# A second mixer in another order: up products first, attention heads between channel slots, state-space heads between output halves

## The chip, the core and the metric

The kernel runs on one core of one Trainium2 chip. The metric is the device time of one execution in microseconds (us). PE is the matrix engine (TensorE), DVE the VectorE, ACT the ScalarE, POOL the GpSimd engine, SP the engine that issues the weight loads.

## The reference

Two transformer blocks follow each other on 256 tokens of width 1024, in float32. The second is the one that matters here:

```
u = rmsnorm(x, norm_mix_w) @ w_in            # z 1024 | xbc 2048 | dt 16 | q_lat 384 | kv_lat 256 | k_rope 32
xbc = silu(causal_conv4(xbc) + b)            # xs 1024 | B 4x128 | C 4x128
y = (C B^T * exp(segment sums of dt*a)) @ (xs*dt)   # 16 state-space heads of 64
y = group_rmsnorm((y + xs*d_skip) * silu(z))
q = rmsnorm(q_lat) @ w_q_up ; k,v = rmsnorm(kv_lat) @ w_kv_up ; rope on 32 of 96 columns
o = softmax(q k^T / sqrt(96), masked by chunks of 64) @ v    # 16 attention heads of 64
x = x + concat(y, o) @ w_out
x = x + memory_attention(rmsnorm(x), rmsnorm(mem)) ; x = x + conv_ffn(rmsnorm(x))
return rmsnorm(x, norm_final_w)
```

The first block has a mixer of its own (differential attention and retention) and a layer of selected experts.

## The kernel before

The tokens are two halves of 128 partitions (t = 0, 1). All weights stand in DRAM as 463 slots of 128x1024 float32, in the order in which they are used (`order`, `SOURCE`). SP loads them into a ring of three (`ring`). ACT casts a slot to its high part (`w_hi`, `hi_parts`, L1292), POOL forms the rest as `w_lo` (L426, in one stage DVE does), and PE computes each product as three matmuls, high by high, high by low and low by high (L458 to L460). `split` counts slots whose `w_lo` is there, `wait_slot` waits for it on PE, and `spent` counts the slots that PE has finished; ACT may overwrite the parts of a slot when the one three before it is spent. So ACT's place of `hi_parts(n)` in its own list of instructions decides when slot n can be used. PSUM has eight banks of 128x512. The order on every engine is written out by hand, with semaphores between engines.

The second mixer runs on PE in this order. Four slots of dt and q latents, four of kv latents and the k_rope columns, eight of z (`panel`). A product that turns the tokens' norm factors into a row (`row_of`), the transposes of the latents (`turn("latents")`). Then 16 slots of xbc by channels: the input h is unscaled, so DVE first multiplies each result by the row of norm factors, then does the four taps of the convolution, and ACT does Silu on it. Transposes of xs and the group products C B^T stand between and behind them. Then 16 state-space heads: `seg_sum` on PE, `clip` on DVE, Exp on ACT, `weigh` on DVE (L2504), three matmuls on PE. Between them stand the up products of q and kv (`up`, 17 units of six 512-column matmuls, nine slots, copied out by ACT and DVE in `up_copied`) and the rotation of q (`rope_products`, `rope_sums` on DVE). Then the transposes of q and k (`qk_turn`), 16 attention heads (`mla_scores`, `masked` on DVE, `mla_exp` on ACT, `mla_turn`, copies, `mla_out`, L1063) with 13 halves of the output product between them (`out_half`, 12 matmuls of 512 columns each, state-space part first), the transposes of the attention output (`out_turn`), and the remaining halves. `add_residual` adds four banks to x on DVE (L1957), and transposes for the next norm follow (L497).

In the last lines DVE multiplies the second half of x by factor and gain as one 128x1024 instruction (L2718) and SP stores it as one transfer of 512 KB, while ACT does the same for the first half.

## Time and profile before

| | us |
|---|---|
| three runs | 1583.86 (median), 1579.18, 1587.04 |
| profiled execution | 1582.71 |
| its span | 1580.6 |
| PE busy | 1508.9 (95%) |
| DVE, ACT, POOL busy | 850.8, 752.0, 971.7 |
| mean granted PE clock | 0.987 |

Busy times are of the span. A matmul's shown length is longer than the distance to the next one's start, since matmuls are pipelined, and so a busy PE isn't a PE at its peak. The second mixer is the stretch from 1064.5 to 1309.9.

### The profile page before, as it was taken

To read this page: it belongs to the slowest core of one execution; us is meant where nothing else is said; L and a number is where in the kernel's file an instruction comes from. 1 tells how busy PE (TensorE), PEld (TensorE's weight loads), DVE (VectorE), ACT (ScalarE), POOL (GpSimd) and SP (SyncE) were. 2 spreads that over 40 slices of the span, in tenths; PEclk is the share of its full clock that TensorE was granted. 3 is DMA by queue.
4 is the path that set the end of the run, shared out by engine and by line. 5 is a ranking of instruction groups with operands and counts; after the bars stand their busy time and mean duration, and the time that the engine had idled before them with its cause. 6 is when DMAs were issued, how large, how long until landed. Compare 5 with 4: busy or idle time off the path is not lost.

```text
span 1580.6 us, 26597 instructions
## 1 busy us (share of the span) xinstructions
PE 1508.9 (95%) x9602; PEld 1354.5 (86%) x9602; DVE 850.8 (54%) x2090; ACT 752.0 (48%) x1248; POOL 971.7 (61%) x412
## 2 busy tenths in 40 slices
PE   7998999999999999999999999979997999999997
PEld 6677999989998888899999999968975878899996
DVE  4555289999996655422222222255776523365665
ACT  6465545544444545444444444455435545544443
POOL 7547888855553000288888888877741155588885
PEclk9999999999999999999999999999997999999999
DMA  7334556543335566565555555554521044355553
GB/s 248 122 105 140 180 180 234 187 134 108 121 108 160 187 195 192 181 187 187 187 187 186 186 186 186 186 196 152 185 83 51 28 173 148 120 163 186 185 185 119
DMA packets 69200, 254.15 MB, mean 161 GB/s; under 512 B 7744, under 2 KB 8000, under 8 KB 68480
## 3 DMA queue, kind: packets, MB, share of 16 engines
q1 hardware_dynamic: 67104, 244.35, 48.6%
q10 hardware_dynamic: 1584, 6.68, 1.2%
q0 software_dynamic: 432, 2.07, 0.3%
q8 instruction: 50, 0.82, 0.2%
q14 instruction: 30, 0.25, 0.0%
HBM read 249.91 MB, written 3.15 MB: 160 GB/s over the span
## 4 chain that ended last, share of the span: by engine, by line
PE 31%; issue 31%; POOL 27%; DVE 8%; POOLq 1%; DMA 1%; ACT 0%; DVEq 0%; ACTq 0%
POOL w_lo L426 27%; PE bank L458 9%; PE bank L459 9%; PE bank L460 9%; PE bank L851 4%; DVE arena L2219 1%; DVE arena L2216 1%; DVE arena L2218 1%; DMA ring<-weights_in 1%; DVE arena L2217 1%; DVE arena L2287 1%; DVE arena L2285 1%; DVE arena L2288 1%; DVE arena L2215 1%; POOLq L436 0%
## 5 line engine op out<-in xcount | busy, mean ns | idle before, releaser
L426 POOL TENSOR_TENSOR w_lo<-ring,w_hi 128x1024 fp32r<-128x1024 f32 x403 | 968.4, 2406 | 593.3 <-ACT w_hi L1292 586.2
L1292 ACT CAST w_hi<-ring 128x1024 fp32r<-128x1024 f32 x460 | 482.4, 1050 | 639.3 <-PE bank L460 595.4
L458 PE MATMUL bank<-h_hi,w_hi 128*128 128x256 f32 x1696 | 487.5, 287 | 5.4 <-ACT arena L1780 2.3
L460 PE MATMUL bank<-h_hi,w_lo 128*128 128x256 f32 x1696 | 480.4, 283 | 0.0
L459 PE MATMUL bank<-h_lo,w_hi 128*128 128x256 f32 x1696 | 480.3, 283 | 0.0
L458 PEld LDWEIGHTS bank<-h_hi,w_hi 128*128 128x128 f32 x1696 | 325.4, 192 | 10.3 <-POOL w_lo L426 2.6
L459 PEld LDWEIGHTS bank<-h_lo,w_hi 128*128 128x128 f32 x1696 | 325.5, 192 | 3.6
L460 PEld LDWEIGHTS bank<-h_hi,w_lo 128*128 128x128 f32 x1696 | 325.2, 192 | 0.0
L458 PE MATMUL bank<-w_hi,act_hi 128*128 128x512 f32 x600 | 235.0, 392 | 4.6 <-DVE act_lo L2372 1.7
L459 PE MATMUL bank<-w_lo,act_hi 128*128 128x512 f32 x600 | 234.5, 391 | 0.0
L460 PE MATMUL bank<-w_hi,act_lo 128*128 128x512 f32 x600 | 233.5, 389 | 0.0
L2367 DVE TENSOR_TENSOR bank<-bank,arena 128x256 f32<-128x256 f32 x68 | 29.4, 433 | 278.2 <-ACT bank L1598 278.1
L458 PEld LDWEIGHTS bank<-w_hi,act_hi 128*128 128x128 f32 x600 | 113.0, 188 | 27.0 <-issue 4.0
L460 PEld LDWEIGHTS bank<-w_hi,act_lo 128*128 128x128 f32 x600 | 112.7, 188 | 24.3
L459 PEld LDWEIGHTS bank<-w_lo,act_hi 128*128 128x128 f32 x600 | 113.0, 188 | 20.1
L2341 DVE TENSOR_TENSOR w_lo<-ring,w_hi 128x1024 fp32r<-128x1024 f32 x60 | 73.5, 1225 | 67.4 <-ACT w_hi L1292 67.2
L458 PE MATMUL bank<-w_hi,h_hi 128*128 128x512 f32 (+2 forms) x224 | 92.9, 415 | 16.7 <-POOL w_lo L426 13.5
L460 PE MATMUL bank<-w_hi,h_lo 128*128 128x512 f32 (+2 forms) x224 | 87.5, 390 | 0.0
L459 PE MATMUL bank<-w_lo,h_hi 128*128 128x512 f32 (+2 forms) x224 | 87.4, 390 | 0.0
L2310 DVE TENSOR_SCALAR work<-bank,chosen_t 128x128 f32<-128x128 f32 x256 | 86.9, 401 | 0.0
L458 PEld LDWEIGHTS bank<-w_hi,h_hi 128*128 128x128 f32 x224 | 43.5, 194 | 31.7 <-POOL w_lo L426 19.0
L851 PE MATMUL bank<-work 128*128 128x128 f32 x512 | 67.4, 275 | 0.0
(392 smaller groups left out, 1836.9 us busy)
## 6 DMA issues: line engine op xcount, KB each, us to landing
ring<-weights_in SPq DMA_DIRECT2D x463, 512.0 KB, 3.5
mem_kv<-arena ACTq DMA_DIRECT2D x2, 1024.0 KB, 7.0
arena<-mem_kv ACTq DMA_DIRECT2D x2, 1024.0 KB, 6.2
xres<-x_in SPq DMA_DIRECT2D x2, 512.0 KB, 6.6
arena<-mem_in POOLq DMA_DIRECT2D x1, 1024.0 KB, 7.9
arena<-rows_in ACTq DMA_DIRECT2D x2, 512.0 KB, 5.2
arena<-consts_in POOLq DMA_DIRECT2D x1, 512.0 KB, 8.7
arena<-consts_in ACTq DMA_DIRECT2D x2, 256.0 KB, 6.3
```

The costliest lines, as they stand in the source:

```text
L426: nc.gpsimd.tensor_tensor(w_lo[:, k, :], ring[:, k, :], w_hi[:, k, :].bitcast(F32), ALU.subtract)\
L458: pe.matmul(out_, a[0], b[0], start=start, stop=False, **kw)
L459: pe.matmul(out_, a[0], b[1], start=False, stop=False, **kw)
L460: return pe.matmul(out_, a[1], b[0], start=False, stop=stop, **kw)
L851: mm = pe.matmul(bank[:, g % 3, i * P:(i + 1) * P], one_hots(2 + u)[:, i, :], one_hots(u)[:, i, :], start=True, stop=True)
L1292: nc.scalar.copy(w_hi[:, k, :], ring[:, k, :]).then_inc(s["hi_made"], 1)
L2215: link(v.max(top[:, 0:8], values))
L2216: v.max_index(index[:, 0:8], top[:, 0:8], values)
L2217: link(v.match_replace(rest, top[:, 0:8], values, -3.0e38))
L2310: v.tensor_scalar(one_hots(u)[:, i, :], iota_p, of(0), of(2), ALU.is_equal, ALU.mult)\
L2341: v.tensor_tensor(w_lo[:, k, :], ring[:, k, :], w_hi[:, k, :].bitcast(F32), ALU.subtract)\
L2367: v.tensor_tensor(a, a, g, ALU.mult).then_inc(s["act_product"], 1)
```

## The change

- The order of the second mixer's slots becomes dt and q, kv and k_rope, z, q_up, kv_up, xbc, output. The channels of xbc come in another order (`XBC`: two of the groups' B and C by turns first, then xs), and in the output product the attention half comes first.
- The latents are transposed between the two panels of z. All 17 up units run one after the other, in banks 6, 7 and 4, 5 by turns. Between the nine of q and the eight of kv PE does 16 transposes of x scaled by its norm factor (`x_mix`, one half scaled by ACT, one by DVE), whose high and low parts (`mix_h`) are the input of the xbc slots. The row of factors and DVE's 16 multiplications by it go.
- Each attention head has one xbc slot between `mla_turn` and `mla_out` (heads 0 to 13; two slots stand ahead), with the group products, transposes of xs and of the attention output at fixed heads (`CB_AT`, `XS_AT`, `OUT_AT`). DVE does the convolution of a slot in each head; ACT does Silu in batches of four at every fourth head. Scores are scaled in ACT's copy of q and masked in PSUM, on 256 columns.
- The state-space heads come last, ten of them with half an output slot of the attention half (`HALF_AT`), six halves follow, then the transposes of y and the 16 halves of the state-space part. y is summed and gated in four groups instead of two halves. The loads of the memory keys and values from DRAM (ACT's queue) move to the eighth state-space head.
- Additions by banks: where PE signalled after two banks of a product, it now signals after banks 0, 1 and 2, and DVE's four additions wait one by one (`residual_half`, four uses, and `mixer_half`).
- First mixer: some of ACT's casts (`hi_parts`) take other places in its list. With `hi_parts(m)` ACT casts all slots up to m that it hasn't cast yet.
- End: squares, gain and factor are done in four pieces of 128x512, and the output goes out in four transfers of 256 KB.

```diff
+XBC = [8, 12, 9, 13, 10, 14, 11, 15] + list(range(8))
...
-    order = ["w_in", "w_out", "mem_k", "queries", "mem_v", "experts", "dt_q", "kv_rope", "z", "xbc", "q_up", "kv_up",
+    order = ["w_in", "w_out", "mem_k", "queries", "mem_v", "experts", "dt_q", "kv_rope", "z", "q_up", "kv_up", "xbc",
...
+        elif name == "xbc":
+            stage(name, [SLOT[name] + j for j in XBC])
+        elif name == "w_out_2":
+            stage(name, [SLOT[name] + (k + KD) % (2 * KD) for k in range(2 * KD)])
...
+XS_AT = {12: (0, 0, 7), 13: (1, 0, 3)}
+OUT_AT = {6: 0, 10: 1, 14: 2}
+HALF_AT = (0, 2, 3, 4, 6, 7, 8, 10, 11, 12)
...
             low("norm_mix", 7)
             panel("z", 0, 512, 0)
-            panel("z", 1, 512, 2)
-            pe.wait_ge(s["mix_scale"], 1)
-            row_of((bank[:, 7, :], 0))
+            pe.wait_ge(s["copied_act"], c0 + 1)
+            pe.wait_ge(s["copied_dve"], d0 + 1)
             pe.wait_ge(s["latents_scaled"], 1)
             turn("latents", lambda b, t: lat[:, t, 16 + b * P:16 + (b + 1) * P] if b < 3 else
                  lat[:, t, 512 + (b - 3) * P:512 + (b - 2) * P], 5, bank0=4)
...
                 name, c, depth, k = UP[i]
-                if k == 0 and i:
-                    before = 3 * (name == "kv_up") + c
-                    pe.wait_ge(s["copied_act"], COPY["q_up"][0] + before)
-                    pe.wait_ge(s["copied_dve"], COPY["q_up"][1] + before)
-                n, half, mm = up_unit(name, c, depth, k, lat_t, 3 * (name == "kv_up"), 512, 6)
...
                 elif i == 2:
                     mm.then_inc(s["up_first"], 1)
-            pe.wait_ge(s["cum_copied"], 1)
-            for i in range(3):
+            for i in range(9):
                 up(i)
-            for g in range(SG):
-                pe.wait_ge(s["xbc_silu"], 13 + g)
-                pe.wait_ge(s["conv_done"], 4 * (13 + g))
+            pe.wait_ge(s["copied_act"], z0 + 4)
+            pe.wait_ge(s["norm_scaled"], SCALED["mix"])
+            turn("mix_h", lambda b, t: x_mix[:, t, b * P:(b + 1) * P], KD)
+            for i in range(9, len(UP)):
+                up(i)
+            adt = area("dts")[:, 0:32].rearrange("p (t h) -> p t h", t=TT)
...
-                if h:
-                    pe.wait_ge(s["mla_masked"], h)
+                if h >= 2:
+                    pe.wait_ge(s["mla_exp"], h - 1)
+                to = 4 - 2 * (h % 2)
...
+            low("mix_h", KD - 1)
+            xbc(0)
+            pe.wait_ge(s["rotated"], TT)
+            pe.wait_ge(s["copied_act"], COPY["kv_up"][0] + 4)
+            pe.wait_ge(s["copied_dve"], COPY["kv_up"][1] + 4)
+            for i in range(4):
+                qk_turn(i, 4 + i)
+            xbc(1)
+            mla_scores(0)
+            mla_scores(1)
+            pe.wait_ge(s["qk_out_act"], 4)
+            for h in range(MH):
+                if h + 2 < MH:
+                    mla_scores(h + 2)
+                mla_turn(h)
+                if 4 + h < MH:
+                    pe.wait_ge(s["qk_out_act"], 4 + h)
+                    qk_turn(4 + h, 7)
+                if 2 + h < 16:
+                    xbc(2 + h)
+                if h == 0:
+                    cum()
+                if h in CB_AT:
+                    cb_product(CB_AT[h])
+                if h in OUT_AT:
+                    pe.wait_ge(s["cb_masked"], (2, 4, 4)[OUT_AT[h]])
+                    if h == 14:
+                        pe.wait_ge(s["xdt_made"], 2)
+                    out_turn(OUT_AT[h], 3)
+                if h in XS_AT:
+                    if h == 12:
+                        pe.wait_ge(s["qk_out_act"], MH)
+                    else:
+                        low("mla_out", 3)
+                    xs_turn(*XS_AT[h])
+                mla_out(h)
...
-                if i == 4 * KD - 2:
-                    mm.then_inc(s["residual_half"], 1)
+                    if k == 2 * KD - 1 and 2 * t + h < 3:
+                        mm.then_inc(s["residual_half"], 1)
...
+            seg_sum(0)
+            seg_sum(1)
+            xs_turn(0, 1, 7)
+            low("mla_out", 5)
+            xs_turn(1, 1, 3)
+            out_turn(3, 2)
...
+            for h in range(SH):
+                if h in HALF_AT:
+                    if done == 1:
+                        low("mla_out", 7)
+                        pe.wait_ge(s["xdt_made"], 4)
+                    out_half(done, m_t)
...
+                if h == 0:
+                    pe.wait_ge(s["xdt_made"], 2)
+                    pe.wait_ge(s["mla_out_copied"], 4)
+                if h == 4:
+                    pe.wait_ge(s["xdt_made"], 4)
+                if h in (8, 12):
+                    pe.wait_ge(s["y_ready"], h // 4 - 1)
...
+                    seg_sum(h + 2)
             while done < 2 * KD:
-                out_half(done, h_t)
+                out_half(done, m_t)
                 done += 1
-            pe.wait_ge(s["mla_out_copied"], 4)
-            out_turn(3, 6)
+            pe.wait_ge(s["y_ready"], SG)
+            pe.wait_ge(s["y_scaled"], 2 * TT)
+            turn("ssd", lambda b, t: xs[:, t, b * P:(b + 1) * P], KD, bank0=4)
             for i in range(2 * KD, 4 * KD):
-                out_half(i, m_t, lambda k: low("mla_out", k))
+                out_half(i, h_t, lambda k: low("ssd", k))
...
-            hi_parts(24 + NS)
+            hi_parts(25 + NS)
...
-            hi_parts(25 + NS)
             mem_k_copied(0)
+            hi_parts(26 + NS)
             act.wait_ge(s["head_mean"], 2)
...
-            hi_parts(26 + NS)
+            hi_parts(27 + NS)
...
-            hi_parts(29 + NS)
+            hi_parts(28 + NS)
...
+            hi_parts(STEP["z"] + 1 + NS)
...
+            act.wait_ge(s["norm_factor"], NORMS["mix"] + 1)
+            nc.scalar.mul(x_mix[:, 0, :], xres[:, 0, :], rstd[:, 6:7]).then_inc(s["norm_scaled"], 1)
...
-            turned_hi("latents", lat_t, 5, lambda b: col("q_g", b) if b < 3 else col("kv_g", b - 3), bank0=4)
-            for j in range(16):
-                hi_parts(STEP["xbc"] + j + 1 + NS)
-                act.wait_ge(s["conv_done"], 4 * (j + 1))
-                nc.scalar.activation(xc[:, j, :], xc[:, j, :], ACT.Silu).then_inc(s["xbc_silu"], 1)
-                if j in (10, 14):
-                    b = j // 14
-                    act.wait_ge(s["turned"], TURN["xs"][0] + 2 * b + 1)
-                    nc.scalar.copy(xs[:, 0, b * 512:(b + 1) * 512], bank[:, 7 - 2 * b, :]).then_inc(s["turned_out_act"], 1)
+                if c == 0:
+                    turned_hi("latents", lat_t, 5, lambda b: col("q_g", b) if b < 3 else col("kv_g", b - 3), bank0=4)
...
+            for p in range(3):
+                up_copied(p)
+            turned_hi("mix_h", h_t, 4, lambda b: col("mix_g", b))
+            up_copied(3)
+            turned_hi("mix_h", h_t, 4, lambda b: col("mix_g", 4 + b), first=4, skip=4)
+            for p in range(4, 7):
+                up_copied(p)
...
+            M = STEP["xbc"] + NS
+            hi_parts(M + 1)
+            for i in range(4):
+                qk_out(i, 4 + i)
+            nc.scalar.activation(warm[:, 6:7], ident[:, 0:1], ACT.Exp)
+            hi_parts(M + 2)
             mla_exp(0)
             mla_exp(1)
             for h in range(MH):
+                if 4 + h < MH:
+                    qk_out(4 + h, 7)
                 if h + 2 < MH:
                     mla_exp(h + 2)
-                if 4 + h < MH:
-                    qk_out(4 + h, 7)
-                if h == 1:
-                    turned_hi("ssd", h_t, KD, lambda b: col("ssd_g", b))
-                if h >= 3:
-                    hi_parts(STEP["w_out_2"] + (h - 3) // 2 + NS)
...
+                if h % 4 == 3:
+                    for pos in range(h - 3, h + 1):
+                        act.wait_ge(s["conv_done"], 4 * (pos + 1))
+                        x = xc[:, XBC[pos], :]
+                        nc.scalar.activation(x, x, ACT.Silu).then_inc(s["xbc_silu"], 1)
+                if 2 + h < 16:
+                    hi_parts(M + 3 + h)
+                if h in OUT_AT:
+                    out_hi(OUT_AT[h], 3)
...
+            O = STEP["w_out_2"] + NS
+            done = 0
+            for h in range(SH):
+                act.wait_ge(s["seg_clipped"], 2 * (h + 1))
+                b = bank[:, 4 + h % 2, 0:3 * P]
+                nc.scalar.activation(b, b, ACT.Exp).then_inc(s["seg_exp"], 1)
+                if h == 0:
+                    out_hi(3, 2)
+                if h in HALF_AT:
+                    hi_parts(O + done // 2)
+                    done += 1
+                if h in (6, 10, 14):
+                    y_squares((h - 6) // 4)
+                if h == 7:
+                    act.wait_ge(s["xdt_made"], 4)
+                    act.dma_start(area("mk_t"), mem_kv[:, 0, :]).then_inc(s["mem_kv_loaded"], 16)
+                    act.dma_start(area("mv"), mem_kv[:, 1, :]).then_inc(s["mem_kv_loaded"], 16)
...
+            hi_parts(O + 8)
+            turned_hi("ssd", h_t, KD, lambda b: col("ssd_g", b), bank0=4)
...
+            piece = lambda a, i: a[:, i // 2, i % 2 * 512:i % 2 * 512 + 512]
+            for i in range(4):
+                act.wait_ge(s["residual_added"], 4 * USE["ffn"] + i + 1)
+                nc.scalar.activation(squares[:, i % 2 * 512:i % 2 * 512 + 512], piece(xres, i), ACT.Square, scale=0.03125,
+                                     accum_out=ssq[:, i:i + 1]).then_inc(s["norm_summed"], 1)
+                act.wait_ge(s["norm_summed"], 2 * NORMS["final2"] + i + 1)
+            act.wait_ge(s["norm_mean"], NORMS["final2"] + 1)
+            nc.scalar.activation(rstd[:, 4:6], ssq[:, 4:6], ACT.Sqrt).then_inc(s["norm_rooted"], 1)
...
-            act.wait_ge(s["gained"], 1)
-            nc.scalar.mul(out_sb[:, 0, :], out_sb[:, 0, :], rstd[:, 2:3]).then_inc(s["out_ready"], 1)
-            act.wait_ge(s["out_ready"], 1)
-            act.dma_start(out[:, 0, :], out_sb[:, 0, :]).then_inc(s["out_stored"], 16)
-            act.wait_ge(s["out_stored"], 32)
+            for n, i in enumerate((2, 0)):
+                nc.scalar.mul(piece(out_sb, i), piece(out_sb, i), rstd[:, 6 + i // 2:7 + i // 2]).then_inc(s["out_ready"], 1)
+                act.wait_ge(s["out_ready"], n + 1)
+                act.dma_start(piece(out, i), piece(out_sb, i)).then_inc(s["out_stored"], 16)
+            act.wait_ge(s["out_stored"], 64)
...
                     for h in range(2):
+                        if 2 * t + h < 3:
+                            dve.wait_ge(s["residual_half"], 3 * use + 2 * t + h + 1)
+                        else:
+                            dve.wait_ge(s["spent"], spent)
                         v.tensor_tensor(xres[:, t, h * 512:(h + 1) * 512], xres[:, t, h * 512:(h + 1) * 512],
                                         bank[:, 2 * t + h, :], ALU.add).then_inc(s["residual_added"], 1)
...
+            v.tensor_scalar(x_mix[:, 1, :], xres[:, 1, :], rstd[:, 7:8], None, ALU.mult).then_inc(s["norm_scaled"], 1)
...
+            for p in range(3):
+                up_copied(p)
+            mix_lo(0)
+            mix_lo(1)
+            rope_products(0)
+            up_copied(3)
+            rope_sums(0)
+            mix_lo(2)
+            mix_lo(3)
+            up_copied(4)
+            rope_products(1)
+            rope_sums(1)
+            up_copied(5)
+            up_copied(6)
...
+                b = bank[:, 4 - 2 * (h % 2), :]
+                causal = b.rearrange("p (t c) -> p t c", t=TT)[:, :, 0:P]
+                v.tensor_tensor(causal, causal, mask.unsqueeze(1).broadcast_to([P, TT, P]), ALU.add).then_inc(s["mla_masked"], 1)
                 dve.wait_ge(s["mla_masked"], h + 1)
...
+            def conv(pos):
+                j = XBC[pos]
+                dve.wait_ge(s["spent"], STEP["xbc"] + pos + 1)
+                b = bank[:, pos % 2, :]
+                v.tensor_scalar(xc[:, j, :], b[:, 0:T], col("xw", 4 * j + 3), col("xb", j), ALU.mult, ALU.add)\
+                    .then_inc(s["conv_done"], 1)
+                for d in range(1, 4):
+                    dve.wait_ge(s["conv_done"], 4 * pos + d)
+                    v.scalar_tensor_tensor(out=xc[:, j, d:T], in0=b[:, 0:T - d], scalar=col("xw", 4 * j + 3 - d),
+                                           in1=xc[:, j, d:T], op0=ALU.mult, op1=ALU.add).then_inc(s["conv_done"], 1)
...
+                if h - 1 in OUT_AT:
+                    out_lo(OUT_AT[h - 1], 3)
+                if 1 + h < 16:
+                    conv(1 + h)
+                if h == 0:
+                    dve.wait_ge(s["cum_done"], 1)
+                    v.tensor_copy(dts[:, 64:96], bank[:, 3, 0:32])
+                    v.tensor_copy(area("cum_t")[0:SH, :], bank[0:SH, 3, T:2 * T]).then_inc(s["cum_copied"], 1)
+                if h in CB_AT:
+                    cb_mask(CB_AT[h])
+                if h in XS_AT:
+                    xs_out(h - 12, *XS_AT[h])
...
+                dve.wait_ge(s["ssd_out"], 4 * g + 4)
+                b = bank[:, 6 + g % 2, :].rearrange("p (t c) -> p t c", t=TT)
+                a = xs[:, :, g * 256:(g + 1) * 256]
+                link(v.tensor_tensor(b, b, a, ALU.add))
+                v.tensor_tensor(a, b, z[:, :, g * 256:(g + 1) * 256], ALU.mult).then_inc(s["y_ready"], 1)
...
+                if h == 0:
+                    xs_out(3, 1, 1, 3)
+                    out_lo(3, 2)
+                    dve.wait_ge(s["xdt_made"], 4)
+                if h in (5, 9, 13):
+                    y_group((h - 5) // 4)
...
+            piece = lambda a, i: a[:, i // 2, i % 2 * 512:i % 2 * 512 + 512]
+            gain = lambda i: area("final_g")[:, i % 2 * 512:i % 2 * 512 + 512]
+            for i in (2, 0):
+                v.tensor_tensor(piece(out_sb, i), piece(xres, i), gain(i), ALU.mult).then_inc(s["gained"], 1)
+            dve.wait_ge(s["norm_summed"], 2 * NORMS["final2"] + 4)
...
+            for i in (3, 1):
+                v.scalar_tensor_tensor(out=piece(out_sb, i), in0=piece(xres, i), scalar=rstd[:, 6 + i // 2:7 + i // 2], in1=gain(i),
+                                       op0=ALU.mult, op1=ALU.mult).then_inc(s["half_ready"], 1)
```

## Rows read from the trace of the kernel before

**Rows 1.** The page, first line.

```profile
span 1580.6 us, 26597 instructions
```

**Rows 2.** Windows by stage: length, busy time (instructions) by engine, granted clock, DMA share, GB/s.

```profile
1064.50:1094.00 29.50, 26.34 (x111) 21.43 (x111) 10.71 (x24) 17.39 (x28) 21.47 (x10) 0.88 0.51 166
1094.00:1146.90 52.90, 49.78 (x414) 48.92 (x411) 42.58 (x91) 26.23 (x41) 40.37 (x17) 1.00 0.55 170
1146.90:1207.50 60.60, 53.18 (x246) 40.36 (x247) 43.15 (x99) 24.38 (x47) 22.19 (x10) 0.95 0.27 85
1207.50:1235.20 27.70, 20.99 (x103) 17.72 (x104) 15.18 (x35) 15.86 (x49) 0.00 (x0) 0.68 0.01 5
1235.20:1285.70 50.50, 48.62 (x301) 41.37 (x300) 24.01 (x60) 22.61 (x65) 14.32 (x6) 1.00 0.20 63
1285.70:1309.90 24.20, 22.62 (x100) 17.92 (x98) 1.96 (x4) 11.32 (x13) 20.36 (x9) 1.00 0.69 243
```

**Rows 3.** Timeline of PE in an attention head: start, duration, instructions.

```profile
1241.00 0.88 PE L1063 MATMUL bank<-arena,work 128*128 128x64 f32 x6 [0.44 <-DVE work L2605]
...
1243.11 0.48 PE L458 MATMUL bank<-w_hi,h_hi 128*128 128x512 f32 x1
1243.43 0.40 PE L459 MATMUL bank<-w_lo,h_hi 128*128 128x512 f32 x1
1243.66 0.40 PE L460 MATMUL bank<-w_hi,h_lo 128*128 128x512 f32 x1
```

**Rows 4.** Waits, 1020 to 1300: total us, times, longest.

```profile
PE bank L458 <- POOL w_lo L426: 11.7, 10, 3.2
```

**Rows 5.** Windows of the lower clock, columns as in rows 2.

```profile
1214.80:1228.70 13.90, 12.15 (x48) 9.91 (x47) 6.06 (x16) 8.46 (x26) 0.00 (x0) 0.51 0.00 0
```

**Rows 6.** Timeline of PE behind the output product.

```profile
1311.40 1.20 PE L497 MATMUL bank<-cst,xres 128*128 128x128 f32 x9 [0.27 <-DVE xres L1957]
```

**Rows 7.** Timeline of PE among z's first slots.

```profile
1076.06 0.79 PE L458 MATMUL bank<-w_hi,h_hi 128*128 128x512 f32 x1 [3.16 <-POOL w_lo L426]
```

**Rows 8.** Timeline of ACT ahead of it.

```profile
1069.48 1.28 ACT L1659 ACT_TABLE_LOAD   x1
1070.77 0.23 ACT L1659 ACTIVATE arena<-arena 128x32 f32<-128x32 f32 x1
...
1072.56 2.92 ACT L1292 CAST w_hi<-ring 128x1024 fp32r<-128x1024 f32 x3
```

**Rows 9.** Timeline of DVE, the rotation of k.

```profile
1073.49 0.17 DVE L1982 TENSOR_TENSOR arena<-arena,rope 128x16 f32<-128x16 f32 x1
1073.69 2.35 DVE L1983 TENSOR_TENSOR arena<-arena 128x16 f32<-128x16 f32 x1
```

**Rows 10.** Timeline of POOL at that time.

```profile
1073.66 7.20 POOL L426 TENSOR_TENSOR w_lo<-ring,w_hi 128x1024 fp32r<-128x1024 f32 x3 [4.58 <-ACT w_hi L1292]
```

**Rows 11.** Timeline of DVE in the state-space heads.

```profile
1203.51 0.62 DVE L2504 TENSOR_TENSOR arena<-bank,arena 128x256 f32<-128x256 f32 x2 [1.30 <-ACT bank L1709]
1204.04 0.88 DVE L2494 TENSOR_SCALAR bank<-bank,arena 128x128 f32<-128x128 f32 x2
1205.49 0.62 DVE L2504 TENSOR_TENSOR arena<-bank,arena 128x256 f32<-128x256 f32 x2 [0.57 <-ACT bank L1709]
```

**Rows 12.** Timeline of PE, a state-space head until the next unit.

```profile
1198.31 0.43 PE L1022 MATMUL bank<-arena 128*128 128x64 f32 x2 [2.22 <-DVE arena L2504]
...
1199.75 0.50 PE L458 MATMUL bank<-w_hi,lat_hi 128*128 128x512 f32 x1
```

**Rows 13.** Waits in the first mixer, 110 to 150.

```profile
PE bank L458 <- POOL w_lo L426: 2.5, 1, 2.5
...
PE bank L458 <- DVE h_lo L1914: 2.0, 1, 2.0
```

**Rows 14.** Timeline of DVE: the additions, and the last instruction.

```profile
1308.70 2.65 DVE L1957 TENSOR_TENSOR xres<-xres,bank 128x512 f32<-128x512 f32 x4 [19.37 <-PE bank L460]
...
1574.98 1.28 DVE L2718 SCALAR_TENSOR_TENSOR arena<-xres,rstd,arena 128x1024 f32<-128x1024 f32 x1
```

521 lines of the change are left out of this document (219 added, 302 removed).

## The prediction

> **How the profile was read, and what bounds the kernel.** First the page: the span of the profiled execution is 1580.6 us [rows 1], and that execution took 1582.71 us, so 2.1 us lie outside the span. It is 1.15 us under the median of the three runs, 1583.86. I work against its time, and the prediction needs no correction beyond that. 0.5% is 7.9 us: a median under 1576.0 counts as faster, one over 1591.8 as slower.
>
> Then the table by stages of the second mixer, which the change rewrites [rows 2]: dt, kv, rope and z until 1094.0, the 16 channel (xbc) slots until 1146.9, the state-space heads with the up products until 1207.5, the passage to attention until 1235.2, the attention heads with output halves until 1285.7, the rest of the output product until 1309.9. In each, PE is the busiest engine, yet it is busy for 221.5 of 245.4 us. What is to be had is what PE loses, and it loses in three ways:
> - Idle: 3.2, 3.1, 7.4, 6.7, 1.9 and 1.6 us by stage, 23.9 in all [rows 2].
> - Restarts. Running 512-column matmuls start 0.23 apart though each is shown for 0.40, so each stop costs about 0.16 more [rows 3]. PE stops some 25 times, for POOL, DVE or ACT (ten times for POOL in the stretch of [rows 4]): 4.0.
> - Half clock. The stretch at 1214.8 was granted 0.51, the lower level, 1.2 GHz [rows 5]. From the mean grants 0.88, 0.95 and 0.68 [rows 2], the time at that level is 2 x 0.12 x 29.5 + 2 x 0.05 x 60.6 + 2 x 0.32 x 27.7 = 30.9 us, and with PE busy 0.76 to 0.89 of it, half of that work was lost: 3.2 + 2.7 + 6.7 = 12.6. Ahead of the 1214.8 stretch PE waited for DVE again and again.
>
> Losses before: 40.5. The mixer's work at full speed is then 245.4 - 40.5 = 204.9.
>
> **The change in the second mixer.** Work added on PE: 16 transposes of the scaled x and no row product, 1.8 - 0.6 = +1.2 (nine transposes are shown for 1.20, of which about 0.3 is the last one's own length: 0.11 each [rows 6]; the row product is estimated at five such matmuls). The sum now asks what PE loses in the new order.
>
> *Up to z's fourth slot.* PE waited 3.16 for POOL at 1076.06 [rows 7], because ACT did Exp and Ln with two table loads ahead of three casts [rows 8], and POOL stood without w_hi. The change puts two casts first, so this wait goes. The two loads (1.28 each) and the new scaling of x now delay a later slot; PE, 2.73 a slot (12 x 0.228) against POOL's 2.40, has won 0.3 a slot by then. Left: 1.6 (0 to 3.2).
>
> *Up products alone, 17 units.* A unit is six matmuls, 1.37; with the transposes 25 us for nine slots, and POOL needs 9 x 2.40 = 21.6, so it keeps up, barely. Formerly the same units filled the waits of the state-space heads. What is late next is DVE: copies, mix_lo and both rope halves stand in one queue, and PE needs its copies for the bank of two units on. 1.3 for that. The rope sums and products read two SBUF tiles; one such small op takes 0.17, and 2.35 when it met POOL's w_lo [rows 9, 10]. Of twelve I let two meet it where PE waits, 1.5 each. Left: 4.3 (0 to the rival below).
>
> The Trainium skill, page "SBUF — State Buffer", section "Who interferes with whom", says that a VectorE instruction with two SBUF inputs and a GpSimd instruction reading SBUF hold each other off for a whole instruction. The 2.35 beside 0.17 agrees. It speaks against putting rope beside nine w_lo in a row, and is what rival B stands on.
>
> *Attention heads with an xbc slot each.* PE: a head is 2.11 (1241.00 to 1243.11), a slot is 24 matmuls of 256 columns, half of 0.23 each and rounded up to 0.12, 2.88 [rows 3]: 4.99. DVE: the heads with halves took 24.01/16 = 1.50, the slots 42.58/16 = 2.66 [rows 2], 4.2 together, and 3.7 without the row scaling, one of a slot's five operations (0.5 at most). ACT: 22.61/16 + 26.23/16 = 3.05, and with eight more table loads (two for each batch of four Silus) 8 x 1.28/16 = 0.64: 3.7. POOL 2.4. So PE sets the pace, and the 3.1 idle of the slots and the 1.9 of the heads go. At the first head the chain scores, mask, maxima, exp has little cover: 2.0 (0 to 4).
>
> The Trainium skill, page "ScalarE: Activation LUTs", section "What ACT_TABLE_LOAD costs", adds to each load a drain of about its own length. In this trace the next activation comes right behind the load and nothing stands before it, 1069.48 to 1070.77 [rows 8]. By the page ACT would be at 4.4 a head instead of 3.7, and the sum stays what it is.
>
> *From the last head to state space.* Heads 14 and 15 have no slot: 2.11 on PE against about 3.7 on DVE and ACT, twice 1.6: 3.2. Then DVE has a queue: two clips (0.88 each), the division and two products for xs (0.66 each, as the bank-wide additions of [rows 14]) and the first weigh (0.62), 4.4, and ACT's hand-over, 1.30 [rows 11]. Against these 5.7 PE has twelve transposes (1.3) and one half (2.7): 1.7 is open, and about 1.1 for the transposes that wait for the division. Left 6.0 (2 to 9).
>
> *State-space heads with halves.* PE alone takes 1.44 a head (1198.31 to 1199.75) [rows 12], DVE 1.98 (1203.51 to 1205.49) [rows 11]. Ten heads have a half, 2.73 more on PE, and are PE's. The other six are DVE's: 6 x 0.54 = 3.2. The group sums (two operations, 1.3) stand in front of the next weigh three times: 3.9. Head 0's extra DVE work past its half: 0.7. Left 7.8 (3 to 12).
>
> *The state-space half of the product last.* Six halves (16.4) now lie between the last head and the turn, and hide the norm (squares, root, factor, scaling) whose place was in the 6.7 idle of 1207.5 to 1235.2. If that cover were gone, some 5 would come back. Left 0.7.
>
> *Clock.* The long stretches at the lower level stood where PE waited in short steps, in the two passages. One such, 7 us long at busy 0.85, is put in for the passage to state space: 3.0 (0 to 7).
>
> Losses after, restarts in them: 1.6 + 4.3 + 2.0 + 6.0 + 7.8 + 0.7 + 3.0 = 25.4. Change in the mixer: 25.4 + 1.2 - 40.5 = -13.9.
>
> *Costed at nothing:* the order of the slots in DRAM and the ring (the same loads in another order); the loads of memory keys and values moved to the eighth state-space head, which compete with at most five weight loads while the DMA engines were busy 0.20 and 0.69 of the last two stages [rows 2]; q scaled in ACT's copy (same instruction); the mask on 256 columns instead of 384 (off PE's path, in DVE's 3.7).
>
> **The other parts.** *First mixer:* casts for the slots ahead are moved in front of ACT's waits. PE waits there 2.5 for POOL once and 2.0 for DVE's h_lo once [rows 13]. If both went 4.5 would come, but h_lo waits on the same ACT, one cast later: -3.0 (-4.5 to +1, a cast of 1.05 in front of what PE waits for). *Additions by bank, five places:* DVE adds 4 x 0.66 (2.65 from 1308.70), PE waits 0.27 behind it [rows 6, 14]. Now bank 1's add needn't wait for bank 0's pair and bank 2's starts a quarter earlier; at three boundaries a turn follows at once: -0.8 (0 to -1.5). *Tail:* the last product by DVE is 1.28 at 1024 wide, and the DMA waits for all of it [rows 14]; by halves 0.64 of it is hidden behind the first transfer, and squares by pieces save some more, while four signals cost some: -0.9 (0 to -1.5).
>
> **Sum.** -13.9 - 3.0 - 0.8 - 0.9 = -18.6: span 1562.0, time 1564.1.
>
> **Rivals.**
> A, the new stalls are mostly absent (chance 0.18). For it: PE's six stages of before had only 1.6 to 7.4 idle each. Passage 2 and not 6, state-space heads 4 and not 7.8, first head 1, up products 1: 12.1 less, and about 2 from the clock: 1550.
> D, DVE or ACT paces the attention heads (0.08). Each head has four hand-overs PE, DVE, ACT, PE, and two batches of Silu stand in ACT's queue before a cast that POOL and so the slot wait for. At 5.9 a head instead of 4.99, 14 heads: +12.6, 1577. Against it: the sums 3.7 and 3.7.
> B, the port (0.04): all twelve rope operations meet a w_lo and PE waits for all: 12 x 2.2 - 3.0 = +23.4, 1587.5. Against it: with POOL idle they run at full speed, and before, one or two in a row met it, not all. It would take ten waits more than the two counted to undo the gain.
> C, the clock, on the slower side (0.05): PE falls to the lower level in the passage to state space, and waits for DVE in six of 16 heads keep it there to the end of the six further halves. 16 x 1.44 + 10 x 2.73 + 6 x 2.73 = 66.7 of work; at half clock it takes as much again, less the stalls (7.8) and clock loss (3.0) already counted, and less about a fifth as ten heads have long busy runs: +40, 1604. It decides from 20 us of full-speed work done at half clock beyond what is counted. For it: 1214.8 to 1228.7 was such a passage [rows 5]; against: there PE had no product, and with halves (1235.2 on) the grant was 1.00 [rows 2].
> That the change does nothing: not possible for 40 us of reordered losses, but gain and loss may cancel; it lies in D and B.
>
> **Chances and range.** Forecast 0.65, A 0.18, D 0.08, C 0.05, B 0.04. The forecast's own range follows from its bounds taken together in part: 1556 to 1573. Over all, 1546 to 1580 leaves out C, B, the lower third of A and the far ends of the rest, under 2 in 10. Faster: forecast and A, 0.83. Within: D and B, and some of what reaches past the forecast's end, 0.10. Slower: C and the end of B, 0.07.
>
> **What would show it.** Right: no 3 us wait for POOL at z's first slots, a shorter one near its fifth; attention heads with a slot 5.0 apart and PE over 0.95 busy; a gap of 4 to 8 us and a drop of the grant before the first state-space head; heads without a half 2 apart, later after a group sum; the mixer from the dt slots to the last half about 231.5 long. Wrong: heads 5.5 or more apart with PE waiting for DVE or ACT (D); rope operations of 2.4 with PE behind them (B); a grant near 0.5 over the state-space heads (C); an up-product stage with POOL as PE's releaser.

## The result: 1559.86 us, 1.6% faster

| | before | changed |
|---|---|---|
| median (lowest to highest) | 1583.04 (1579.18 to 1587.04), 4 runs | 1559.86 (1555.44 to 1560.11), 4 runs |
| profiled execution, its span | 1582.71, 1580.6 | 1555.44, 1553.6 |

The ratio is 0.9844, with a 95% interval of 0.9826 to 0.9862. That is 22 to 28 us less; 18.6 were forecast. By the rule of 0.5% in the prediction it counts as faster. The profiled execution of the changed kernel was its fastest, so differences between the two traces flatter it by some us, and the experiments below take that apart.

Windows by stage of the changed kernel: until the second panel of z, the up products, the attention heads with xbc slots, the state-space heads with halves, the rest of the output product (columns as in [rows 2]):

```profile
1059.30:1088.90 29.60, 28.60 (x129) 23.26 (x130) 14.11 (x31) 22.84 (x37) 25.27 (x11) 1.00 0.59 185
1088.90:1114.00 25.10, 23.61 (x125) 19.89 (x124) 15.96 (x31) 14.80 (x27) 20.70 (x9) 1.00 0.61 188
1114.00:1205.00 91.00, 87.35 (x684) 82.97 (x683) 65.66 (x154) 57.82 (x129) 38.31 (x17) 0.98 0.32 99
1205.00:1255.00 50.00, 47.53 (x215) 36.71 (x214) 30.97 (x80) 19.03 (x43) 12.51 (x6) 0.86 0.28 95
1255.00:1283.00 28.00, 27.20 (x128) 22.52 (x127) 7.96 (x13) 14.15 (x23) 22.52 (x10) 1.00 0.50 154
```

The five windows are 223.70 long and PE is busy in 214.29 of it. The same stretch took 245.4 [rows 2]. PE's idle time in it is 9.4, where it was 23.9. Its waits from the last up units on, grouped:

```profile
PE bank L1153 <- DVE arena L2660: 2.5, 2, 1.4
PE bank L1036 <- ACT work L1754: 1.6, 1, 1.6
PE bank L1056 <- DVE work L2629: 1.3, 1, 1.3
PE bank L1066 <- issue: 0.8, 1, 0.8
PE bank L470 <- DVE h_lo L1978: 0.8, 1, 0.8
```

And the two of the stages before, among z's slots and at the fifth panel of the up products, in PE's timeline:

```profile
1072.86 0.50 PE L470 MATMUL bank<-w_hi,h_hi 128*128 128x512 f32 x1 [0.88 <-POOL w_lo L438]
...
1107.63 0.47 PE L470 MATMUL bank<-w_hi,lat_hi 128*128 128x512 f32 x1 [1.42 <-issue]
```

An attention head with its slot is 4.96 long, from one `mla_out` to the next (4.99 forecast), and there is no gap between. The heads that also have a group product or transposes of the attention output are 5.40 to 5.84 long:

```profile
1137.29 0.78 PE L1056 MATMUL bank<-arena,work 128*128 128x64 f32 x6
1137.90 0.87 PE L1036 MATMUL bank<-arena 96*128 96x128 f32 x4
...
1142.25 0.78 PE L1056 MATMUL bank<-arena,work 128*128 128x64 f32 x6
```

What was not so small is the clock. Windows of the changed kernel: the passage to state space, two heads later, the last heads, and the stretch behind the first memory query product:

```profile
1200.00:1208.00 8.00, 6.91 (x25) 5.44 (x26) 6.08 (x16) 4.73 (x10) 0.00 (x0) 0.60 0.21 66
1220.00:1228.00 8.00, 8.00 (x35) 6.11 (x33) 5.30 (x14) 3.36 (x9) 2.36 (x1) 0.79 0.39 131
1244.00:1252.00 8.00, 6.30 (x22) 5.29 (x23) 3.59 (x10) 4.72 (x12) 2.38 (x1) 0.62 0.03 7
1293.00:1298.00 5.00, 3.95 (x21) 3.95 (x22) 0.00 (x0) 1.95 (x3) 4.19 (x2) 0.66 0.33 94
```

In the mixer 17 us ran at the lower level (31 before). The last row is new: PE waits 2.27 there as before, and here the grant fell for 3.4 us behind it. The stretch from the additions behind the output product to the next ones is 68.52 in this trace. Of the thirteen traces of the changed kernel and its variants, four have this fall and are 68.52 to 68.63 long there. Eight others are 67.13 to 67.17, and the one with the old additions, without the fall, is 67.74, as before. So 1.4 of the gain were given back.

The grant didn't only fall behind stops. In the middle of the state-space heads it fell while PE was busy all the time:

```profile
1222.00:1224.00 2.00, 2.00 (x6) 1.59 (x5) 1.87 (x5) 1.59 (x6) 1.21 (x1) 0.52 0.00 0
```

### The profile page after: what moved, and what is told of

Same layout as the page of the kernel before. It is cut to its first block, busy times and chain, and to the rows that moved or that the text cites. A ratio compares the mean times of both kernels' runs of the same rounds, so it can differ in the third digit from the quotient of the medians.

```text
span 1553.6 us, 26642 instructions
## 1 busy us (share of the span) xinstructions
PE 1500.3 (97%) x9614; PEld 1351.3 (87%) x9614; DVE 848.3 (55%) x2085; ACT 763.1 (49%) x1267; POOL 972.1 (63%) x412
## 4 chain that ended last, share of the span: by engine, by line
PE 31%; issue 30%; POOL 28%; DVE 8%; POOLq 1%; DMA 1%; ACT 1%; DVEq 0%; ACTq 0%
POOL w_lo L438 28%; PE bank L470 9%; PE bank L471 9%; PE bank L472 9%; PE bank L861 4%; DVE arena L2283 1%; DVE arena L2280 1%; DVE arena L2282 1%; DVE arena L2281 1%; DMA ring<-weights_in 1%; DVE arena L2351 1%; DVE arena L2349 1%; DVE arena L2352 1%; DVE arena L2279 1%; POOLq L448 0%
## 5 line engine op out<-in xcount | busy, mean ns | idle before, releaser
L470 PE MATMUL bank<-w_hi,h_hi 128*128 128x512 f32 (+2 forms) x224 | 89.5, 400 | 13.5 <-POOL w_lo L438 11.0
```

Of the source, the lines that this page charges most:

```text
L470: pe.matmul(out_, a[0], b[0], start=start, stop=False, **kw)
```

## The experiments

An execution of one and the same kernel varies by up to 10 us here, more than most edits are worth. So each profiled execution is also cut at marks that all kernels have: the first addition behind the first mixer, those ahead of and behind the second mixer, and so on. "The mixer" below is the stretch from DVE's additions ahead of the second mixer's norm to those behind its output product: 272.85 in the trace of before, 251.19 in that of the changed kernel. The time at the lower clock is twice the missing grant times the length, and the idle time is the sum of PE's gaps. Each ratio is against runs of the kernel before made in the same group, whose medians are 1582.68 to 1584.6; across groups the ratios compare better than the times.

### The changed kernel again, and its three small parts undone

> The changed kernel again, as the base of this group. The theory of the trace: its profiled execution (1555.44) was its fastest, and in the others one stretch more is done at the lower clock, so the median comes out near 1559 and the ratio to the kernel before near 0.984. If the profiled execution was typical and the others disturbed, the median is near 1556.

Measured: 1561.09 (1552.05 to 1562.69), ratio 0.9851 (0.9825 to 0.9878). The first profiled execution was a lucky one, as the first theory said. The profiled execution of this group has a span of 1558.9, and 27.3 us of its mixer at the lower clock where the first had 17.1.

Casts of the first mixer in their old places:

```diff
-            hi_parts(25 + NS)
+            hi_parts(24 + NS)
...
-            mem_k_copied(0)
-            hi_parts(26 + NS)
+            hi_parts(25 + NS)
+            mem_k_copied(0)
...
-            hi_parts(27 + NS)
+            hi_parts(26 + NS)
...
-            hi_parts(28 + NS)
+            hi_parts(29 + NS)
```

> Only the order of ACT's casts in the first mixer is put back. Theory: that order is worth what the two traces differ by at the end of the first mixer, 3.8 us, so this kernel is 3 to 4.5 us slower than the changed one. Rival: of the 3.8 a part is clock (0.95 against 1.00 granted there) that comes and goes by execution, and only the 2.1 of idle time is the order's: 2 us slower.

Measured: 1559.83, ratio 0.9861 (0.9838 to 0.9884), no difference that the times can tell. The traces tell it. The additions behind the first mixer start at 146.39; in the changed kernel's trace at 143.22, and at 142.75 to 145.04 in all twelve with the new order. PE's waits in that mixer with the old places, and then in the changed kernel:

```profile
PE bank L470 <- POOL w_lo L438: 2.5, 1, 2.5
PE bank L470 <- DVE h_lo L1978: 1.7, 1, 1.7
```

```profile
PE bank L697 <- DVE arena L2232: 1.2, 1, 1.2
PE bank L470 <- POOL w_lo L438: 1.1, 1, 1.1
```

4.2 of waits against 2.3. The order is worth 3.2 by these two traces, of which 1.9 is waits and the rest clock and restarts: the old order's trace has 3.4 us at the lower clock there. The trace of before has the old order too. Its additions start at 147.52, of which 0.7 is the wait for a second bank, so 146.8 is the number to compare. Against the mean of the twelve traces with the new order, 143.5, the two old ones are 3.1 later, and single pairs differ by 1.3 to 4.1.

Additions with the old waits:

```diff
-                        if 2 * t + h < 3:
-                            dve.wait_ge(s["residual_half"], 3 * use + 2 * t + h + 1)
+                        if t == 0:
+                            dve.wait_ge(s["residual_half"], 3 * use + 2)
```

> Only the additions wait as before (banks 0 and 1 for bank 1, banks 2 and 3 for the last). Theory: 0.27 of PE's wait at each of three boundaries comes back, 0.8 us slower, at most 1.5. Rival: the wait in front of the second half of the transposes is paid by nobody else, and it is 0 to 0.3.

Measured: 1556.57, ratio 0.9845 (0.9821 to 0.9869). Again only the marks tell: from the additions behind the output product to those behind memory attention 67.74 against 67.15 in the run beside it, from there to the last additions 193.92 against 193.31, and from PE's last matmul to the end 9.53 against 8.97 (8.97 in the first trace too, and 9.26 before; the expectations' 8.94 and 9.31 come from spans rounded to 0.1). So it is 0.6 at each of three places, 1.8 in all. The edit changes two more places, at the end of the first mixer and of the experts. The stretches there differ by 2 us and more from trace to trace, so nothing can be read from them. PE's last product and the transposes behind memory attention, in the changed kernel:

```profile
1351.31 0.39 PE L472 MATMUL bank<-w_hi,m_lo 128*128 128x512 f32 x1
1351.54 2.14 PE L509 MATMUL bank<-cst,xres 128*128 128x128 f32 x16
```

All 16 transposes run through, where nine of them waited 0.27 for DVE [rows 6]. The 0.27 was only part of it: the first seven had also stood apart.

The end as before, in two pieces (SP's part of the edit; ACT's squares and scaling and DVE's gain and factor go back with it):

```diff
-            for n, i in enumerate((3, 1)):
-                sp.wait_ge(s["half_ready"], n + 1)
-                sp.dma_start(out[:, i // 2, i % 2 * 512:i % 2 * 512 + 512], ...
+            sp.wait_ge(s["gained"], 2)
+            sp.dma_start(out[:, 1, :], out_sb[:, 1, :]).then_inc(s["out_stored"], 16)
```

> Only the last part is put back: gain, factor and transfer in two pieces of 512 KB. Theory by the two traces: from the start of PE's last matmul to the end of the span it was 9.31 us before and 8.94 after, so 0.4 slower. The prediction's term was 0.9. Rival: the four smaller transfers cost as much as they gain, 0.

Measured: 1557.59, ratio 0.9833 (0.9808 to 0.9858). From PE's last matmul to the end 8.67, against 8.97 with four pieces: the pieces cost 0.30, and what the end gained it gained from the additions. The last rows of ACT in the changed kernel show where:

```profile
1547.84 0.72 ACT L1933 ACTIVATE arena<-arena,rstd 128x512 f32<-128x512 f32 x1 [0.29 <-DVE rstd L2810]
1548.59 0.36 ACTq L1935 DMA_DIRECT2D out<-arena  x1
1549.00 0.72 ACT L1933 ACTIVATE arena<-arena,rstd 128x512 f32<-128x512 f32 x1 [0.44 <-ACT arena L1933]
1549.75 0.34 ACTq L1935 DMA_DIRECT2D out<-arena  x1
```

ACT scales one piece, issues its transfer, and only then scales the other. The last transfer leaves 5.09 after PE's last matmul began (1544.66); before it was 5.00 (1576.29 and 1571.29). This trace of the two-piece end also had the mixer at 252.67, with a stop of 3.76 among the up products in place of 1.42. That was the lead for the third group.

### Stops and the clock in the state-space heads

Two more halves among the heads, ahead of the matmuls of heads 13 and 14, so that four remain behind them:

```diff
-HALF_AT = (0, 2, 3, 4, 6, 7, 8, 10, 11, 12)
+HALF_AT = (0, 2, 3, 4, 6, 7, 8, 10, 11, 12, 13, 14)
```

> Two of the six halves that stood behind the state-space heads move to heads 13 and 14, where PE stopped for DVE's weigh (1.39 and about 0.9). Theory 1, the lower clock follows such stops: both stops go and with them the stretch of about 7 us at the lower clock that began at the second in all five traces, so the stretch from the additions before the mixer to those behind it shrinks by 2.3 + 3 = 5 us. Theory 2, the clock falls with the thin matmuls of these heads, stops or not: only the 2.3 of the stops, and a stretch at the lower clock stands there as before. Rival to both: with four halves left the norm of the state-space output is late and PE waits up to 2 us at its transposes.

Measured: 1554.56 (1551.41 to 1559.45), ratio 0.9822 (0.9794 to 0.985). PE's timeline of the changed kernel at the last two heads, 14 and 15, and then the windows of this one there:

```profile
1244.62 0.43 PE L1153 MATMUL bank<-arena 128*128 128x64 f32 x2 [1.40 <-DVE arena L2660]
...
1246.58 0.69 PE L1153 MATMUL bank<-arena 128*128 128x64 f32 x2 [1.08 <-DVE arena L2660]
...
1248.89 0.63 PE L472 MATMUL bank<-w_hi,m_lo 128*128 128x512 f32 x1
```

```profile
1240.00:1248.00 8.00, 8.00 (x39) 6.02 (x39) 5.45 (x14) 3.37 (x8) 3.61 (x2) 1.00 0.34 81
1248.00:1256.00 8.00, 7.16 (x37) 5.74 (x35) 5.06 (x8) 6.13 (x15) 2.40 (x1) 1.00 0.12 51
```

A 512-column matmul shown for 0.63 is one at the lower level. Both stops are gone and so is the stretch of 6.8 us at that level, which began at or between the two stops in each of the ten traces that have them. It is absent in all three traces that have the halves there. From the first matmul of head 12 to the additions behind the output product, the same work took 40.24 to 41.05 in the ten (mean 40.53) and 36.56 or 36.57 in the three. That is 4.0 less: more than theory 2's 2.3, and near theory 1's 5 with the rival's wait taken off. That wait came, but small: 1.57 at the transposes, where it was 0.79. Of the 4.0 the stops are 1.2 (2.2 gone in the mean, 1.0 new), and the 2.8 that are left are what 6.8 us of lower clock cost. So the clock came back with the stops. What isn't separated: the edit also puts wide matmuls between the thin ones of these heads, and a run of thin matmuls together with a stop could do the same as the stop alone.

Stops aren't the whole rule either. In six of the thirteen traces the grant fell once more among the first state-space heads, for 3.4 to 13.7 us, with no stop of over 0.15 directly ahead (one is the row at 1222.00 above). What brings that is open.

Three edits ahead of these heads: the convolution of the last slot goes behind DVE's last copy, the second transposes of xs to bank 7 (three waits of PE that go with it are left out here), and an up copy ahead of two low parts.

```diff
-XS_AT = {12: (0, 0, 7), 13: (1, 0, 3)}
+XS_AT = {12: (0, 0, 7), 13: (1, 0, 7)}
...
-                if 1 + h < 16:
-                    conv(1 + h)
+                if h < 14 or h == 15:
+                    conv(min(1 + h, 15))
...
+            up_copied(4)
             mix_lo(2)
             mix_lo(3)
-            up_copied(4)
```

> Three edits that take away stops ahead of the state-space heads: DVE does the last convolution behind the last copy (stop of 1.26), the second xs transposes go to bank 7 and so the transposes of the attention output needn't wait for DVE (stop of 0.83), and DVE copies an up product ahead of two low parts (stop of 1.43, in one trace 3.76). Theory 1 (stops bring the lower clock): 3.5 us by the stops and 3 to 6 by the clock behind the passage. Theory 2: the 3.5 alone, the stretch at the lower clock in the first state-space heads stays.

Measured: 1561.02 (1554.07 to 1569.31), ratio 0.9849 (0.9816 to 0.9882): neither theory. The stops of the passage moved instead of going (0.83 and 1.25 became 0.82, 0.65 and 0.96), so whether the clock there follows them was not tested. The worst stop was 6.00, at the transposes of q and k behind the up products, instead of 1.42 among them.

> Both together, and the end (gain, factor, transfer) as before in two pieces of 512 KB, which by the traces is 0.26 shorter (8.71 against 8.97 from PE's last matmul to the end). Theory 1: -5 -6.5 -0.3, near 1547 and under 0.978 of the kernel before. Theory 2: -2.3 -3.5 -0.3, near 1553.

Measured: 1556.35 (1551.97 to 1561.17), ratio 0.9832 (0.9805 to 0.9858); the grant stayed at 1.00 over the last heads here too, and the passage kept three stops (0.82, 0.65 and 1.27) and 6.8 us at the lower level. A miss as a whole: no better than the two halves alone.

### What paces the attention heads

Silu in each head (`if True: for pos in (h,):` in place of `if h % 4 == 3: for pos in range(h - 3, h + 1):`).

> Silu of a slot in every attention head instead of four in every fourth: the same activations, and ACT changes its function table 32 times for the 8 of the changed kernel. ACT has 3.05 of work a head and now two loads. By the row (1.28 a load, no drain) 3.05 + 2.56 = 5.6 a head, 0.6 over PE's 4.97: 16 x 0.6, about 10 us slower. By the page of the Trainium skill, ScalarE: Activation LUTs, 2.66 a switch, an estimate: 3.05 + 5.32 = 8.4 a head, 54 us slower. If ACT's queue is no chain at all but is hidden by the two heads that it runs ahead: 0.

Measured: 1563.7 (1558.41 to 1566.92), ratio 0.9867 (0.9829 to 0.9905). Windows over the same 77 us of heads, first this kernel and then the changed one:

```profile
1127.70:1204.70 77.00, 76.16 (x612) 73.43 (x613) 57.44 (x133) 72.72 (x129) 31.75 (x14) 1.00 0.29 90
```

```profile
1121.20:1198.20 77.00, 76.14 (x611) 73.43 (x612) 57.20 (x133) 46.76 (x108) 32.69 (x15) 1.00 0.31 97
```

The heads are as long as in the changed kernel (69.01 from the first `mla_out` to the fourteenth in both), and ACT is busy 26.0 more for 21 more loads, 27 instead of 6, 1.24 each. My 3.05 of other ACT work was too much: it is 46.76 in the 77 us, 3.0 a head with the loads. So even the crowded ACT, 4.7 a head, stayed under PE's 4.97. At 2.66 a switch, the figure of the Trainium skill (ScalarE: Activation LUTs, What ACT_TABLE_LOAD costs), the 21 loads would have brought ACT to 46.76 + 55.9 = 103 us in a stretch of 77, an estimate. The measurement decides: the row's 1.28 is the whole price here.

More DVE work in each slot's convolution, one and then five operations (range(1), range(5)), each written where nobody reads:

```diff
+                for i in range(5):
+                    v.tensor_scalar(arena[:, 26624 + i * T:26624 + (i + 1) * T] if i < 4 else work[:, 0:T], b[:, 0:T],
+                                    col("xw", 4 * j + 3), col("xb", j), ALU.mult, ALU.add)
```

> One more DVE operation on 256 columns in each slot's convolution, written where nobody reads, as a stand-in for the row scaling that the change removed. DVE is busy 3.6 of 4.97 us a head. Theory: the removed scaling was worth nothing on DVE's side, 0 to 0.5 us. Rival D (a chain through DVE sets the pace): 16 x 0.45 = 7 us slower.

Measured: 1561.07, ratio 0.9846 (0.9816 to 0.9876); the heads are unchanged, again 69.01 from the first `mla_out` to the fourteenth, and the two stops in heads 14 and 15 grew from 0.83 and 1.25 to 1.73 and 1.70. Removing the row scaling thus gave nothing in the heads with a slot and about 1.3 behind them.

> Five more such operations a slot: DVE 3.6 + 5 x 0.5 = 6.1 a head. If DVE's busy time is what counts, heads are 6.1 apart instead of 4.97: 14 x 1.1 = 16 us slower. If a chain over PE, DVE and ACT counts (the copy in front of the output stands in the same queue), more, up to 14 x 2.5 = 35.

Measured: 1576.4 (1570.26 to 1583.58), ratio 0.9956 (0.9932 to 0.998). From the first head's stop to the last one's it is 96.0 against 79.9, 16.1 more, as DVE's busy time would have it (16), and far from the chain's 35. Of it 11.1 stand between the first `mla_out` and the fourteenth, 0.85 a head, and 5 behind them, where DVE is late. Over 77 us of these heads DVE is busy for 73.74:

```profile
1122.10:1199.10 77.00, 70.33 (x539) 65.18 (x540) 73.74 (x173) 43.49 (x98) 28.40 (x13) 1.00 0.28 83
```

So DVE's busy time counts, not the chain. Rival D would start near 4.97 of DVE work a head, by this reading; the changed kernel has 3.7.

### The rotation beside POOL

Eleven traces now had a stop between the first up product and the first attention head (the expectation below counts ten, and five for six in its middle group). The longest was 1.4 four times, 2.5 to 3.8 six times, 6.0 once. DVE and POOL in the kernel with 6.0:

```profile
1111.63 2.63 DVE L2537 TENSOR_TENSOR arena<-arena,rope 128x256 f32<-128x256 f32 x1
1114.18 2.60 DVE L2538 TENSOR_TENSOR arena<-arena,rope 128x256 f32<-128x256 f32 x1
1116.70 0.41 DVE L2539 TENSOR_TENSOR arena<-arena,rope 128x256 f32<-128x256 f32 x1
1117.15 2.58 DVE L2542 TENSOR_TENSOR arena<-arena 128x256 f32<-128x256 f32 x1
```

```profile
1108.78 7.72 POOL L438 TENSOR_TENSOR w_lo<-ring,w_hi 128x1024 fp32r<-128x1024 f32 x3 [0.49 <-ACT w_hi L1327]
1117.11 2.34 POOL L438 TENSOR_TENSOR w_lo<-ring,w_hi 128x1024 fp32r<-128x1024 f32 x1 [0.61 <-ACT w_hi L1327]
```

The three long operations start 0.04 to 0.35 behind the start of a w_lo and end just behind its end. In the changed kernel's trace there were two, 1.85 and 2.63, and a third of 0.71 that started 0.43 ahead of a w_lo's end. Only the 1.85 and the 0.71 stand ahead of the stop of 1.42; the 2.63 begins at 1107.77, when the stop is over. In the four traces with 1.4 it is the same, and where a second long one stands ahead of the stop it is 2.5 or more. Each of the eleven has two to four long ones, not up to five as the expectation says. The next kernel leaves out the rotation of q:

> The changed kernel without the rotation of q: its twelve DVE operations in the up products are left out (q stays unrotated). In ten traces so far two to five of the twelve ran 1.8 to 2.7 us instead of 0.41, and PE stopped there for 1.4 (four traces), 2.5 to 3.8 (five) and 6.0 us (one). If these stops are the port's, PE stops nowhere between the first up product and the first attention head, and the stretch from additions to additions is shorter by those 1.4 to 3.8, mean 2.7, and by the clock behind them. If the stops are DVE's plain work, leaving out 12 x 0.41 = 4.9 of it takes away the 1.4 but POOL's share stays the same: no more than 1.4.

Measured: 1555.61 (1550.46 to 1556.74), ratio 0.9813 (0.9793 to 0.9833). The stop is gone, the mixer is 248.60 at the same 17.1 us of lower clock as the first trace (251.19), and idle is 2.1 less. This alone doesn't tell the port from DVE's plain work, since both went; the next kernel does.

The last kernel has the 12 halves, the two-piece end (both left out here), and the second operand of each sum in PSUM:

```diff
-            tmp = lambda i: squares[:, i * 256:(i + 1) * 256].rearrange(...
+            tmp = lambda i, t: (bank[:, 2 * t, i // 2 * 256:i // 2 * 256 + 256] if i % 2 else squares[:, i * 256:(i + 1) * 256]).rearrange(...
...
+                dve.wait_ge(s["lo_made"], LOW["mix_h"] + 4 * t + 2)
```

> A version meant to be faster: 12 halves among the heads, the end in two pieces, and two of the rotation's four products written to free banks, so that each of the four sums reads one operand from PSUM and one from SBUF. Theory (two SBUF operands are what meets POOL): the four sums take 0.42 to 0.45 each in place of up to 2.7, the first of them too, which took 1.8 in every trace; the products may still meet. Then one long operation fewer than in the other traces and a stop at the fifth up panel of 0 to 2.4. Rival: any DVE operation that touches SBUF meets POOL, and the sums are as long as before. Time by the theory 1553, ratio 0.981.

Measured: 1552.91 (1549.04 to 1554.81), ratio 0.9796 (0.9778 to 0.9815), the lowest of all, though its interval overlaps that of the 12 halves alone (0.9794 to 0.985). DVE and POOL in it:

```profile
1104.15 0.41 DVE L2534 TENSOR_TENSOR arena<-arena,bank 128x256 f32<-128x256 f32 x1
1104.47 0.42 DVE L2535 TENSOR_TENSOR arena<-arena,bank 128x256 f32<-128x256 f32 x1
...
1107.28 1.61 DVE L2528 TENSOR_TENSOR arena<-arena,rope 128x256 f32<-128x256 f32 x1
1108.82 2.63 DVE L2529 TENSOR_TENSOR bank<-arena,rope 128x256 f32<-128x256 f32 x1
```

```profile
1103.26 2.44 POOL L436 TENSOR_TENSOR w_lo<-ring,w_hi 128x1024 fp32r<-128x1024 f32 x1 [1.12 <-ACT w_hi L1324]
1106.21 4.95 POOL L436 TENSOR_TENSOR w_lo<-ring,w_hi 128x1024 fp32r<-128x1024 f32 x2 [0.50 <-ACT w_hi L1324]
```

The sums run in 0.41 in the middle of a w_lo, and the products, with both operands in SBUF, still wait. The stop of 1.4 at the fifth up panel is gone, though DVE does the same twelve operations. So it came from the long first sum. One stop is left, 1.29 at the transposes of q and k, behind the two long products.

## Why the prediction was right

The direction and the place were right, and so was the main mechanism: PE sets the pace of the new stages, and its idle time goes. The time lies in the range, 4 us under the forecast. The sizes inside the mixer were less good. The new order itself was not undone piece by piece; that the idle time went with it, stage by stage, is read from the two traces. Point by point:

- z: 1.6 forecast, 0.88 measured; the 3.16 went, as said. No run tests ACT's new order there by itself.
- Up products: 4.3 forecast; 1.4 in four traces, 2.5 to 6.0 in seven. Two of the twelve operations meeting a w_lo for long was right for the changed kernel, but only one of them where PE waits. Rival B is real and stays small: of the eleven traces none had more than four long ones.
- Attention heads: 4.99 against 4.96; first head 2.0 against 1.56. DVE at 3.7 was right, ACT at 3.7 was 3.0.
- Passage: 6.0 forecast, 0.83 + 1.25 = 2.1. Both stops stand in heads 14 and 15, so of the 3.2 for these heads 2.1 came. The step that failed is the other 2.8, for DVE's queue ahead of the first state-space heads. In the first trace it cost nothing, while PE did its transposes there at the lower clock. In `same_again`, where the grant fell only later, PE waited there for DVE's division:

```profile
1207.87 1.11 PE L1066 MATMUL bank<-cst,arena 128*128 128x128 f32 x4 [1.21 <-DVE arena L2581]
```

So at full clock 1.2 of the 2.8 came (two variants had 0.50 and 1.21 there). At the lower clock PE's own transposes took longer and covered the wait, so the two losses don't add.
- State-space heads: 7.8 forecast, 1.40 + 1.08 = 2.5. This step failed too. I charged each of the six heads without a half 0.54 and each group sum 1.3. DVE needs 1.98 where a head with a half gives it 4.2, and runs ahead in them. Heads 1, 5, 9 and 13, said to be 2 apart, follow 1.33 behind the one before without a stop, and PE waits only in the last two, where two more heads without a half follow a group sum.
- Turn: 0.7 against 0.79.
- Clock: 3.0 forecast, for one stretch of 7 us. Between a trace with 34.1 us at the lower level (mixer less idle 240.1) and one with 6.8 (229.0) each such us costs 0.40, and the 3.4 us behind the first memory query product cost 1.4, the same price. The changed kernel has 13.7 to 27.3 in five traces with its mixer, 5.5 to 11, and 17.1 in the first, 6.8.
- Mixer in all: -13.9 forecast; -21.7 by the first trace, and 252.4 as the mean of five against 272.85, -20.4. Idle gave 14.3 of the 21.7, the clock (30.7 to 17.1 us) 5.4, and 2.0 are left for restarts.
- First mixer: -3.0 forecast, -3.1 by the means. Additions: -0.8 forecast for five places, -1.8 at three. End: -0.9 forecast for the pieces, +0.30; this step had the sign wrong, since the hidden half of DVE's last product is outweighed by ACT's second piece, which waits for the first one's transfer to be issued.

So the stalls of the passage and of the state-space heads were sized 9 us too large together, and the clock 4 too small. That these errors partly cancel is luck, and so is part of the small miss in the time. Of the signs for being right, three didn't come: the gap of 4 to 8 us ahead of the first state-space head, heads without a half 2 apart, and a mixer of 231.5 (223.7 measured). One sign of rival B did come, rotation operations of 2.6 with PE behind them. Rival A (chance 0.18) described the stalls better than the forecast did, and its 2 us of clock gain is what failed in it. Rival C didn't happen: the grant fell in the passage and came back in the heads with halves. Of before there is one trace, so how much of the 5.4 by the clock is luck of that one stays open. Its mean grant of 0.987 lies inside the 0.981 to 0.990 of the executions of before in the groups of experiments.

## What to carry to other kernels

Engines that work one or two rounds apart don't pay for each short round: cost a wait where several short rounds of the leader come together, and put filler work there rather than spread evenly. A stop of the matrix engine can be worth more than its length, when a stretch at half clock comes with it: with two stops of 2.0 to 2.5 us together came 6.8 us at half speed, 2.7 more by the 0.40 above. And a wait priced for full clock can vanish where the clock is low: don't add the two. When runs vary by more than an edit is worth, cut the traces at common marks and compare stretch by stretch.

## What the runs showed of the hardware

- Five traces with the same second mixer spent 13.7 to 27.3 us of it at the lower clock. The clock is most of the spread of the times: the execution of 1552.05 had a mean grant of 0.994 and that of 1562.69 one of 0.986, and 0.008 of 1560 us is 25 us at the lower level, 10 us at the price of 0.40 (an estimate). Of two traces of the very same kernel, the stop of 2.27 behind the first memory query product was followed by a lower grant in one and by 1.00 in the other.
- A DVE operation with both operands in SBUF waited for POOL's running w_lo to end (2.63 for 0.41), as the Trainium skill has it (SBUF — State Buffer, Who interferes with whom), and the same operation with one operand in PSUM did not (0.41 in the middle of one). Which operations meet changed among kernels that are the same up to this place. POOL is held up as well: where a rotation operation ran in 0.41 right at the start of a w_lo (1107.44 in the changed kernel's trace), that w_lo took 2.70 in place of 2.40.
- Table loads cost ACT 1.28 and nothing beside it, 27 of them in 77 us.
